# Gate matmuls one column block ahead of the merge, and the last stage's sums on VectorE with the scaling a tile behind

## The reference, cut to what matters

```python
h = rmsnorm(x, norm_mix_w[l])
proj = h @ w_in[l]          # ..., ga, gr are its last 2 x 2048 columns
...
mix = jax.nn.sigmoid(ga) * (o_a @ w_branch_moba[l]) + jax.nn.sigmoid(gr) * (y_r @ w_branch_ret[l])
x = x + mix @ w_out[l]
h = rmsnorm(x, norm_ffn_w[l]).reshape(B * S, D)
y = hierarchical_moe(h, ...)      # top-1 group, top-2 experts in it
x = x + y.reshape(B, S, D)
...
return rmsnorm(x, norm_final_w)
```

## Time and profile before

| | |
|---|---|
| median of 3 runs | 4065.7 us (4064.14 to 4392.77) |
| profiled execution, its own time | 4065.84 us |
| its span, core 4, the slowest | 4064.4 us |
| spans of cores 0 to 7 | 4061.1, 4038.6, 4027.1, 4056.3, 4064.4, 4032.5, 4021.9, 4054.0 us |
| mean granted TensorE clock, cores 0 to 7 | 0.869 to 0.872 of 2.4 GHz |
| busy on core 4 | PE 2868.9 us (71%), DVE 890.2 (22%), ACT 913.3 (22%), POOL 596.8 (15%) |
| gate stage on core 4 | 2031.9 to 2440 us |
| last stage on core 4 | 3967 to 4064.4 us |

### The profile page before, as it was taken

One profiled execution on the slowest core, in us unless ns is written; L12 is line 12 of the kernel. 1 busy time (PEld: TensorE's weight loads), 2 busy tenths in 40 slices (PEclk: granted clock), 3 DMA queues, 4 the chain that ended last, 5 costly groups with the idle time before them and its releaser, 6 DMA issues.

```text
span 4064.4 us, 50883 instructions; the slowest of 8 cores (4021.9 to 4064.4 us)
## 1 busy us (share of the span) xinstructions
PE 2868.9 (71%) x17543; PEld 1616.4 (40%) x17766; DVE 890.2 (22%) x2030; ACT 913.3 (22%) x1679; POOL 596.8 (15%) x637
## 2 busy tenths in 40 slices
PE   1568999989899999999789997415544454555450
PEld 0445555556555555656434443212221222222120
DVE  1443222222222222222201111251110110111015
ACT  1444314141423324141501000111111111111111
POOL 1002111111111110111111110001111111111104
PEclk9789999999999999999899998658777777777775
DMA  8872848576656558485375548749999999999977
GB/s 183 267 258 88 187 156 178 198 134 212 109 190 161 168 187 190 156 179 177 45 135 73 73 57 181 150 127 177 175 176 177 174 177 181 177 179 174 177 195 263
DMA packets 280841, 673.01 MB, mean 166 GB/s; under 512 B 108176, under 2 KB 206864, under 8 KB 247184
## 3 DMA queue, kind: packets, MB, share of 16 engines
q0 software_dynamic: 216688, 318.84, 48.5%
q1 hardware_dynamic: 60160, 327.84, 23.3%
q10 hardware_dynamic: 3744, 23.07, 1.6%
HBM read 1078.07 MB, written 105.91 MB: 291 GB/s over the span
## 4 chain that ended last, share of the span: by engine, by line
PE 53%; DMA 27%; DVE 6%; issue 5%; ACT 4%; another core or an unknown queue 3%; SPq 0%; POOL 0%; DVEq 0%; ACTq 0%; POOLq 0%
DMA s_arena<-weu 11%; PE pb L340 7%; PE pb L468 6%; PE pb L1203 6%; PE pb L814 5%; PE pb L494 4%; DMA s_arena<-h_scr 3%; PE pb L456 3%; DMA s_bufA<-weu 3%; PE pb L714 3%; PE pb L825 3%; PE pb L501 3%; PE pb L731 2%; PE pb L718 2%
## 5 line engine op out<-in xcount | busy, mean ns | idle before, releaser
L1203 PE MATMUL pb<-s_arena,t_XT 128*128 128x512 bf16 x927 | 259.1, 443 | 380.7 <-DMA s_arena<-weu 351.2
L340 PE MATMUL pb<-s_arena 128*128 128x512 bf16 x1712 | 396.3, 387 | 17.3 <-DVE s_arena L446 9.8
L468 PE MATMUL pb<-s_arena 128*128 128x256 bf16 x3072 | 364.5, 281 | 3.0 <-DVE t_U L363 2.5
L468 PEld LDWEIGHTS pb<-s_arena 128*128 128x128 bf16 x3072 | 308.0, 101 | 56.1 <-issue 5.0
L1203 PEld LDWEIGHTS pb<-s_arena,t_XT 128*128 128x128 bf16 x928 | 100.9, 111 | 534.1 <-issue 460.2
L340 PEld LDWEIGHTS pb<-s_arena 128*128 128x128 bf16 x1792 | 176.5, 99 | 218.5 <-issue 28.9
L1207 DVE TENSOR_TENSOR t_actb<-pb,t_silt 128x512 bf16<-128x512 f32 x47 | 32.5, 691 | 979.4 <-PE pb L1215 949.7
L814 PE MATMUL pb<-s_arena 128*128 128x512 bf16 x1004 | 224.7, 382 | 6.5 <-DMA oy_scr<-t_U 5.5
L486 POOL TENSOR_TENSOR t_KZ<-t_t 128x256 bf16<-128x256 f32 x96 | 69.4, 723 | 965.3 <-DVE t_t L483 629.5
L723 ACT ACTIVATE t_N<-pb 128x512 bf16<-128x512 f32 (+1 forms) x368 | 191.3, 527 | 60.7 <-PE pb L731 40.5
L1217 ACT COPY t_actT<-pb 128x512 bf16<-128x512 bf16 x47 | 27.5, 585 | 785.9 <-PE pb L1190 768.1
(11 more groups left out here) (277 smaller groups left out, 3739.6 us busy)
## 6 DMA issues: line engine op xcount, KB each, us to landing
s_arena<-hT_scr SPq DMA_DIRECT2D x56, 2048.0 KB, 9.7
s_arena<-h_scr SPq DMA_DIRECT2D x168, 512.0 KB, 11.2
s_arena<-weg POOLq DMA_DIRECT2D x20, 2048.0 KB
s_arena<-weu POOLq DMA_DIRECT2D x20, 2048.0 KB
s_arena<-wed POOLq DMA_DIRECT2D x19, 2048.0 KB
s_arena<-w_in POOLq DMA_DIRECT2D x32, 1024.0 KB, 32.4
t_U<-xs SPq DMA_DIRECT2D x32, 1024.0 KB, 7.0
s_arena<-rtab SPq DMA_DIRECT2D x48, 512.0 KB, 11.6
```

What stands on the lines that cost most here:

```text
L340: S.op("pe", lambda e: e.matmul(pb[bk][:, :], lhsT=W1b[:, c, col:col + 128], rhs=hti[:, c, :], start=(c == 0), stop=(c == 15)), reads=[b_W ...
L468: S.op("pe", lambda e: e.matmul(pb[bk][:, off:off + 256], lhsT=hTg[gi][:, c, tl * 128:(tl + 1) * 128], rhs=W1b[:, c, 384:640], start=(c == ...
L1203: S.op("pe", lambda e: e.matmul(pb[bk][:, :], lhsT=XT[i][:, c, :], rhs=wv[:, c, :], start=(c == 0), stop=(c == 15)), reads=[b_XT[i][c // 8 ...
```

## The change

In the gate stage, the gate matmuls and sigmoids of block 0 come first (`gates(0)`). In each block `fc` the gate matmuls of block `fc + 1` are issued ahead of the branch matmuls of block `fc`; the sigmoids of block `fc + 1` are issued for each half behind the products and the sum of block `fc`. `load_fc` takes a list of parts: the gate weights of a pair are loaded behind the last gate matmuls that read the buffer, the branch weights behind the last merge that does.

In the last stage both sums of a tile are on VectorE, in place in x, GpSimd does nothing, and the loop is skewed: sums, square and root of tile t (`fin_add`) are issued ahead of reciprocal, scaling and store of tile t - 1 (`fin_out`).

```diff
--- before.py
+++ after.py
@@ -240,11 +240,13 @@
             S.dma("pool", f"wq{off}", W1b[:, :, off:off + wd], w_in[:, col:col + wd].rearrange("(c p) n -> p c n", p=128),
                   writes=b_W1[off // 128:(off + wd) // 128])
 
-    def load_fc(fp):
+    def load_fc(fp, js=(0, 1, 2, 3)):
         k = fp % 2
         s_ = slice(fp * 256, (fp + 1) * 256)
         for j, v in enumerate((w_in[:, 9216 + fp * 256:9216 + (fp + 1) * 256], w_in[:, 11264 + fp * 256:11264 + (fp + 1) * 256],
                                wbm[:, s_], wbr[:, s_])):
+            if j not in js:
+                continue
             S.dma("pool", f"fw{k}_{j}", PWK[k][j][:, :, :], v.rearrange("(c p) n -> p c n", p=128),
                   writes=[b_PW[k][j]] + (b_ring + b_tab if fp == 0 else []))
 
@@ -799,21 +801,42 @@
             sg = [w1f[:, 14336 + 1024 * i:15360 + 1024 * i].bitcast(F32) for i in range(4)]; b_sg = [Buf(f"sg{i}") for i in range(4)]
             tt = [tmp(f"tt{i}", [128, 512]) for i in range(4)]; b_tt = [Buf(f"tt{i}") for i in range(4)]
 
+            def gates(fc):
+                k = (fc // 2) % 2
+                co = (fc % 2) * 128
+                for th in range(2):
+                    base = 4 * th
+                    for j in range(2):
+                        W_ = PWK[k][j]
+                        for c in range(16):
+                            S.op("pe", lambda e: e.matmul(pb[base + j][:, :], lhsT=W_[:, c, co:co + 128], rhs=hTg[th][:, c, :],
+                                                          start=(c == 0), stop=(c == 15)),
+                                 reads=[b_PW[k][j], b_hTo[th]], writes=[b_pb[base + j]])
+                for i in range(4):
+                    S.op("act", lambda e: e.activation(out=sg[i], in_=pb[4 * (i // 2) + i % 2][:, :], func=sig_f),
+                         reads=[b_pb[4 * (i // 2) + i % 2]], writes=[b_sg[i]])
+
+            load_fc(1)
+            gates(0)
             for fc in range(16):
                 k = (fc // 2) % 2
                 co = (fc % 2) * 128
                 Wg1, Wg2, Wm, Wr = PWK[k]
-                if fc % 2 == 0 and fc + 2 < 16:
-                    load_fc(fc // 2 + 1)
+                if fc + 1 < 16:
+                    GQ = fc + 1
+                    kq = (GQ // 2) % 2
+                    cq = (GQ % 2) * 128
+                    for th in range(2):
+                        for j in range(2):
+                            W_ = PWK[kq][j]
+                            for c in range(16):
+                                S.op("pe", lambda e: e.matmul(pb[4 * th + j][:, :], lhsT=W_[:, c, cq:cq + 128], rhs=hTg[th][:, c, :],
+                                                              start=(c == 0), stop=(c == 15)),
+                                     reads=[b_PW[kq][j], b_hTo[th]], writes=[b_pb[4 * th + j]])
+                    if fc % 2 == 0 and fc + 4 < 16 + 2 and fc // 2 + 2 < 8:
+                        load_fc(fc // 2 + 2, (0, 1))
                 if fc == 12:
                     load_wo(0, Wob0, b_Wbf[2])
-                for th in range(2):
-                    base = 4 * th
-                    for j, W_ in ((0, Wg1), (1, Wg2)):
-                        for c in range(16):
-                            S.op("pe", lambda e: e.matmul(pb[base + j][:, :], lhsT=W_[:, c, co:co + 128], rhs=hTg[th][:, c, :],
-                                                          start=(c == 0), stop=(c == 15)),
-                                 reads=[b_PW[k][j], b_hTo[th]], writes=[b_pb[base + j]])
                 for th in range(2):
                     ts_ = slice(th * 512, (th + 1) * 512)
                     st_ = th
@@ -825,14 +848,18 @@
                         S.op("pe", lambda e: e.matmul(pb[base + 3][:, :], lhsT=Wr[:, c, co:co + 128], rhs=YRT[:, c, ts_], start=(c == 0), stop=(c == 15)),
                              reads=[b_PW[k][3], b_YR[c // 8]], writes=[b_pb[base + 3]])
                     i0, i1 = 2 * st_, 2 * st_ + 1
-                    S.op("act", lambda e: e.activation(out=sg[i0], in_=pb[base][:, :], func=sig_f), reads=[b_pb[base]], writes=[b_sg[i0]])
-                    S.op("act", lambda e: e.activation(out=sg[i1], in_=pb[base + 1][:, :], func=sig_f), reads=[b_pb[base + 1]], writes=[b_sg[i1]])
                     S.op("dve", lambda e: e.tensor_tensor(out=tt[i0][:, :], in0=pb[base + 2][:, :], in1=sg[i0], op=ALU.mult),
                          reads=[b_pb[base + 2], b_sg[i0]], writes=[b_tt[i0]])
                     S.op("dve", lambda e: e.tensor_tensor(out=tt[i1][:, :], in0=pb[base + 3][:, :], in1=sg[i1], op=ALU.mult),
                          reads=[b_pb[base + 3], b_sg[i1]], writes=[b_tt[i1]])
                     S.op("pool", lambda e: e.tensor_tensor(out=mixT[:, fc, ts_], in0=tt[i0][:, :], in1=tt[i1][:, :], op=ALU.add),
                          reads=[b_tt[i0], b_tt[i1]], writes=[b_mixT[th]])
+                    if fc + 1 < 16:
+                        for i in (i0, i1):
+                            S.op("act", lambda e: e.activation(out=sg[i], in_=pb[base + i % 2][:, :], func=sig_f),
+                                 reads=[b_pb[base + i % 2]], writes=[b_sg[i]])
+                if fc % 2 == 1 and fc // 2 + 2 < 8:
+                    load_fc(fc // 2 + 2, (2, 3))
             S.barrier()
 
         x_scr = nc.dram_tensor("x_scr", [NOWN, D], F32).ap()
@@ -1300,22 +1327,33 @@
             S.dma("act", f"fz{k1}", y1[k1], y_scr[NOWN + t * 128:NOWN + (t + 1) * 128, :], writes=[b_y1[k1]])
         for t in range(nf - 2):
             fin_load(t)
-        for t in range(8):
-            if t + nf - 2 < 8:
-                fin_load(t + nf - 2)
+        def fin_add(t):
             j = t % 4
             k = t % nf
-            k1 = k
             xa, bx = xfin[t]
-            S.op("pool", lambda e: e.tensor_tensor(out=y1[k1], in0=xa, in1=y1[k1], op=ALU.add),
-                 reads=[bx, b_y1[k1]], writes=[b_y1[k1]])
-            S.op("dve", lambda e: e.tensor_tensor(out=xa, in0=y0[k], in1=y1[k1], op=ALU.add),
-                 reads=[b_y0[k], b_y1[k1]], writes=[bx])
-            rms_tile(xa, bx, junk, b_junk, st, b_st[j], j)
+            for ya, by in ((y0[k], b_y0[k]), (y1[k], b_y1[k])):
+                S.op("dve", lambda e: e.tensor_tensor(out=xa, in0=xa, in1=ya, op=ALU.add), reads=[by, bx], writes=[bx])
+            S.op("act", lambda e: e.activation(out=junk[:, :], in_=xa, func=AF.Square, accum_out=st[:, 2 * j:2 * j + 1]),
+                 reads=[bx], writes=[b_junk, b_st[j]])
+            S.op("act", lambda e: e.activation(out=st[:, 2 * j:2 * j + 1], in_=st[:, 2 * j:2 * j + 1], func=AF.Sqrt, scale=1.0 / D, bias=RMS_EPS),
+                 reads=[b_st[j]], writes=[b_st[j]])
+
+        def fin_out(t):
+            j = t % 4
+            k = t % nf
+            xa, bx = xfin[t]
+            S.op("dve", lambda e: e.reciprocal(out=st[:, 2 * j + 1:2 * j + 2], in_=st[:, 2 * j:2 * j + 1]), reads=[b_st[j]], writes=[b_st[j]])
             S.op("dve", lambda e: e.scalar_tensor_tensor(out=y0[k], in0=xa, scalar=st[:, 2 * j + 1:2 * j + 2],
                                                          in1=nwfB[:, :], op0=ALU.mult, op1=ALU.mult),
                  reads=[bx, b_st[j], b_nwf], writes=[b_y0[k]])
             S.dma("sp", f"out{k}", out[t * 128:(t + 1) * 128, :], y0[k], reads=[b_y0[k]])
+        for t in range(9):
+            if t < 8:
+                if t + nf - 2 < 8:
+                    fin_load(t + nf - 2)
+                fin_add(t)
+            if t >= 1:
+                fin_out(t - 1)
         S.barrier()
     return nc, dbg
```

## The result

| | before | changed |
|---|---|---|
| median | 4065.7 us (3 runs shown ahead of the prediction; 4141.46 us with four more) | 4039.76 us (7 runs) |
| ratio, 95% interval | 1 | 0.9925 (0.9909 to 0.9942) |
| span of the slowest core, profiled | 4064.4 us (core 4) | 4039.2 us (core 3) |

The prediction was 4030.7 us, a ratio of 0.991, with 4020 to 4048 as its range. Some executions of either kernel fall into a slower state of the chip (they lift the median of seven before), and the ratio leaves them out; where a later profile shows one die in it, only the cores named are read. The ratio stands for 30 us; 4065.7 and 4039.76 are 25.9 us apart, the two profiled spans 25.2 us.

What follows compares the result with a forecast made beforehand. The prediction took the expert stage as bound by its weight stream and the stages before it by TensorE. Gate stage 16 us plus last stage 19 us made 35 us: 4065.7 - 35 = 4030.7 us, range 4020 to 4048.

Steps and rivals of the forecast that it cites:

- a reused y0 buffer has a path of its own: Last stage: store 4.1, reload 13.9, adds and scaling 11.7, 30 us against 36 available; 3 us of waiting taken overall.
- Gates ahead: Gate stage: the next block's gate matmuls fill the YRT waits, 16.0 us gained on core 4.
- YRT's second half stays where it landed: Gate stage, block 0: second half still lands at 2066.2 on core 4, leaving 1.1 us to wait.
- margins of the gate banks: Gate stage: banks free 2.0 us behind the branch matmuls, wanted after 5.2 and 6.9 us, so no cost.
- rival 4: Gate stage: gate banks released late stop TensorE in each of 15 blocks; 4076 us at 3 us a block; chance 0.02.
- Between the stages: From wout matmuls through the experts: the earlier start is carried through to the end, nothing lost.
- Rival 2: Expert stage: shared HBM paces the stream, so the gate stage's gain is lost; 4047 us; chance 0.10.
- Last stage: Both sums on VectorE and the skew: 22.3 us gained, less 3 us of waiting for data, taken as 19 us.
- The rhythm: Last stage: VectorE takes 7.2 us per tile, bounds 7.0 and 7.5, where data are there.
- the landing of the first y1: Last stage: y1 of tile 0 lands at 3981.46 on core 4, as before the change.
- The prediction's sentence on that page: Last stage: at about 358 GB/s per core, 23.1 MB end at 4032 and the stage gains 18 us.
- Rival 1: Last stage: mixed traffic stays at 247 GB/s, so loads set the pace; 8 us gained, not 19; 4042 us; chance 0.15.

Runs made afterwards that it cites:

- e9: Changed kernel with the gate weights of the third and later pairs issued one block later; ratio to before 0.9909 (0.9873 to 0.9945).
- e1: Changed gate stage with the last stage of the kernel before; ratio to before 0.9977 (0.9944 to 1.001).
- e2: Gate stage of the kernel before with the changed last stage; ratio to before 0.9963 (0.9946 to 0.9979).
- e7: Changed kernel, but scaling writes over x and the store leaves from there, so no y0 reload waits for a store; ratio to before 0.9923 (0.9901 to 0.9944).
- e11: Changed kernel with the skew kept but the first sum back on GpSimd; no ratio, last stage 89.3 to 91.1 us on late cores.
- e4: Changed kernel without the skew, both sums still on VectorE; no ratio, last stage 97.3 and 98.0 us on late cores.
- e3: Changed kernel with the y0 load of tile t+3 behind the store of tile t-1 on SP; no ratio, last stage 79.5 to 86.7 us on late cores.
- e8: Changed kernel with second-pair branch weights issued later, scaling in place, norm weights behind three y tiles; ratio to before 0.9931 (0.9897 to 0.9965).
- e5: Changed kernel repeated unaltered on another chip; ratio to before 0.9925 (0.9904 to 0.9945).

## Why the prediction was right or wrong

The direction was right, and so were the two mechanisms of the gain, the waits filled in the gate stage and the freed VectorE rhythm in the last: the ratio forecast was 0.991, the measured one 0.9925, which is 30 us where I had 35, and the median is 9 us above the forecast and inside the range. That range was wide enough to take in two rivals. What failed is what I had said of the waits that are left. All three terms of the sum were taken too well, and behind the largest shortfall, the last stage's 14 us for 19, stands a wait whose mechanism the prediction had wrong: that a reused y0 buffer has a path of its own.

*Gates ahead, 16.0 us.* It measured 14.5 us on the slowest core and 14.2 in the mean. The step that failed is that YRT's second half stays where it landed: it came 35.5 to 37.1 us after the first gate matmul in place of 32.9 to 35.1, so the wait left was 2.3 to 3.7 us, not 1.1. e9 puts about 1 us of it down to the new early gate loads, the partner's or the core's own. I had checked the new loads against this core's own queue alone, not against the readback. The margins of the gate banks, the sigmoids' order and the weight loads were right: no idle before L833, and rival 4 did not come.

*Between the stages, 0.* It cost 2.3 us in the mean and 4.1 on the slowest core. The late cores of one execution differ by more (1519.3 to 1526.5 us before), so none of it is shown to be due to the change. Rival 2 in full (16 us lost) is excluded by the profile on the first chip, and by e1 beside e2 on another.

*Last stage, 19 us.* It measured 14.0 us in the mean, 12.7 on the slowest core. The rhythm was right (7.13 us a tile, forecast 7.2), ScalarE was hidden, GpSimd's slowing gone. Two steps failed. First, that "a reused y0 buffer has its own path", with "in sum 30 us against five tiles of 7.2 = 36": the store's 4.1 us came from a stage whose DMA queues had room. DMA issues of the changed kernel's last stage, core 3 (KB each, median us to landing), which answer to the earlier trace rows:

```profile
out<-s_arena SPq DMA_DIRECT2D x4, 1024.0 KB, 10.1
out<-t_ysb SPq DMA_DIRECT2D x4, 1024.0 KB, 8.6
```

And the path isn't one buffer's: on SP the paths of all buffers are strung together, because the next store stands behind the waiting load. I had said of each added wait what is queued behind it on GpSimd, and left SP out; the skew moves the store behind the next tile's load, and that was the queue to look at. e7 shows it: without that wait the 5 to 7 us at tiles 5 to 7 are 0. I had allowed 3; it was 6.2 in the mean, so 3 of the 5 us that are missing are this step's.

Second, the landing of the first y1 was carried over from before, 14.2 us, and came at 16.9. That is 2.8 us; with the 3 above it makes 6 for the 5 that are missing, so the split is rough. The windows from the stage's first load to that landing tell how much a late core and its partner moved (last columns: DMA share, GB/s). Before, core 4 and its partner 5:

```profile
3967.30:3981.50 14.20, 0.00 (x0) 0.00 (x0) 0.00 (x0) 0.00 (x0) 0.04 (x1) 0.50 0.93 347
```

```profile
3967.30:3981.50 14.20, 0.00 (x0) 0.00 (x0) 10.65 (x4) 2.78 (x4) 14.20 (x3) 0.50 0.62 201
```

Changed, core 3 and its partner 2:

```profile
3954.80:3972.40 17.60, 0.00 (x0) 0.00 (x0) 2.34 (x2) 0.00 (x0) 0.00 (x0) 0.50 0.87 271
```

```profile
3954.80:3972.40 17.60, 0.00 (x0) 0.00 (x0) 16.96 (x12) 5.21 (x7) 0.00 (x0) 0.50 0.99 349
```

The early partner, freed of GpSimd's slow adds, moves 349 GB/s in place of 201 just when the late core starts, and the late core gets 271 in place of 347. For cores 0 and 1 the step is smaller: partner 356 in place of 286, late core 289 in place of 322. The kernels agree: with the partner at 221 and 262 GB/s (e11) y1 lands at 14.7 and 15.0 us, with it at 342 and 338 (e4) at 16.7 and 16.1. The other cores agree as well. Over the eleven profiles that load the norm weights first (88 cores, each with the window from its first load to the landing), y1 lands after 13.0 to 14.9 us where the partner moved up to 262 GB/s, and after 15.2 to 18.7 where it moved over 300. It is a correlation, not an experiment on the partner itself. The two sum to 620 GB/s in the changed kernel, 645 for cores 0 and 1.
The Trainium skill, HBM Reference, section Specifications (TRN2), gives 716 GB/s for a pair and about 358 for each of its cores; the partner's 349 is near that share, and the late core stays well under it at a DMA share of 0.87. The prediction's sentence on that page gave 18 us for this stage, nearer to the measured 14 than my 19, but by another mechanism than what e7 showed: the rate did not set those waits.

*Rival 1*, the stage of loads, had the right place and the wrong cause: the loads of tiles 5 to 7 were late by order, not by rate, and that cost about 3 us of the gain, not 11.

## What to carry to other kernels

When a loop is skewed, write out for every queue that issues DMAs what now stands behind what: a load that waits for an older store, ahead of a store that is ready, strings all stores together. Taking the wait away (here a result written in place, from a buffer that is not reloaded) is safer than reordering, since reordered loads came late elsewhere in e3 and e8. Moving an operation off a contended engine and filling a wait are worth little alone and much together, so time them as a pair; and of cores that share memory, the late one's loads must be priced with the early one at its new, faster pace.

## What the runs showed that I had not expected

A late core's first megabytes in the last stage come later the more its partner moves then: 13.2 to 15.3 us to the first y1 with the first sum on GpSimd, 14.5 to 18.8 with it on VectorE and the norm weights loaded first. The early cores, whose partner is still in the expert stage, have it at 13.1 to 13.8 us on the first chip with the changed kernel. But it is the partner's rate that goes with it, not its stage: early core 0 of e11 had 18.8 us, with its partner at 323 GB/s in the expert stage, and four early cores of e3, e5 and e7 had 16.6 to 17.8, with it at 308 to 332. And a dependent pair of VectorE adds of 2048 float32 costs 2.39 us from start to start, against 2.21 for an independent pair (3972.35 to 3974.56 in the changed kernel): 0.18 us more, in this one pair.
